# Recurrence of a hybrid encoder layer: order of the gram products, copies and decays around a chunk's slot, signs folded into copies, whole staging loads

## The chip, the cores and the metric

One Trainium2 chip, one core. The metric is device microseconds of one execution of the whole layer. The engines are TensorE (PE in the profile), VectorE (DVE), ScalarE (ACT), GpSimd (POOL) and SyncE (SP), which here only issues DMAs.

## What is computed

One encoder layer over 2048 tokens of 1024 channels. A combined projection feeds a bidirectional RWKV-7 time mixing (8 heads of 64) and a windowed attention; both are projected back, and a gated feed-forward follows. The change touches the recurrence of the first, which the reference writes step by step, for both directions:

```python
def rwkv7_step(S, inp):
    r, w, k, v, a, b = inp
    sa = jnp.einsum('dbhvk,dbhk->dbhv', S, a)
    S = S * w[..., None, :] + sa[..., None] * b[..., None, :] + v[..., :, None] * k[..., None, :]
    y = jnp.einsum('dbhvk,dbhk->dbhv', S, r)
    return S, y
```

with `a = -kk`, the negated and normalised key, and `b = iclr * kk`.

## The kernel before

The layer is a row of blocks: attention projections and attention, the RWKV projections, the gates, `recurrence_block`, then output projection, up and down. Only `recurrence_block` changes. It does the recurrence in chunks of 64 tokens (`L`), 32 chunks (`NCH`) for each direction `d`; direction 1 runs over the chunks from the back. Two heads lie in the two halves of the partitions, four such pairs (`RU`) side by side, so one tile of 128x256 elements holds a quantity of a chunk.

Inside a chunk the dependence of each token on the earlier ones is a triangular system. Its matrix (the "gram", products of the decayed `kk` with the grown `b`) is cut into 32x32 diagonal blocks and one off-diagonal block. The diagonal blocks of four chunks (`GROUP`), both directions and all heads are collected in `E`, transposed to `W` (`turn`), and solved together: `solve` on POOL makes 31 steps of a product and a sum on `W` and `V` (the first group is solved on DVE). `turn_back` transposes the inverses `V` into `upper` and `lower`. From them ACT's `spread` fills `Z` and `side` of a chunk with the masks `halves`, PE's `cross` and `corner` make the off-diagonal block of the inverse, and DVE's `merge` adds it to `Z`.

The loop `SLOTS` runs from -9 to 31, once on each engine, and the order within a slot is a list of stages written out by hand; each stage is called for both directions. In slot c an engine works on chunk c (`now`: the state work), c+1 (`ahead`: pair products, masks, inverse), c+8 (`front`: grams; `LAG` is 8) and c+9 (`after`: decays and growths). A slot in which c+1 is a multiple of four is called fresh: its chunk c+1 needs the group of inverses that is just being finished. Semaphores counted per stage (`done`) connect the engines.

- SP, `load`: six DMAs per direction bring the gates of chunk c+10 to `inp`; `load_raw` brings raw values to `toks` (only in the run-up, before slot 0), `load_v` the centred values, `store` writes the output.
- ACT: `x_copy`, `u_copy`, `spread`, `decay` (exp of the cumulated sum, to `dec`), `y_copy`, `tok_copy` (transposed keys), `growth`, `cross_copy`, `gram_copy`; in fresh slots `spread` stands after `y_copy`.
- POOL: `keys(f)` multiplies keys by `grow`, then a quarter of `solve`, for f = c+8.
- DVE: `scaled` (to `ar`, and the chunk's end decay to `dec_end`), `mask`, in fresh slots `turn_back`, then `state`, `state_decay`, `diagonal_a`, `diagonal_b`, `turn` once a group, `merge`.
- PE: `x_part`, `pairs_part`, `u_part`, `y_state`, `h_part`, `y_part`, `tok_part`, `cross`, `gram`, `corner`, and in the run-up `v_part`, which centres the raw values.

Of the kernel before, what the change touches and what calls it, by code (L numbers as in the profile page):

```python
# [7 lines left out]
ALU = mybir.AluOpType  # L8
ACT = mybir.ActivationFunctionType
# [12 lines left out]
RU = RW // P  # L22
R_TILES = 14
AH = 8
L = 64
# [11 lines left out]
MASK_COLS = dict(halves=2, both0=128, both1=128, running0=128, running1=128, centre=64)  # L37
# [11 lines left out]
def host_constants():  # L49
# [8 lines left out]
        halves=np.concatenate([s < 32, s >= 32], 1),  # L58
# [1017 lines left out]
def recurrence_block(nc, K):  # L1076
# [15 lines left out]
    LAG = 8  # L1092
# [9 lines left out]
    with ExitStack() as ctx:  # L1102
# [26 lines left out]
        raw_v = lambda d, r: toks[d][:, :, r % 2]  # L1129
# [81 lines left out]
        with nc.Block() as block:  # L1211
            @block.sync
            def _(sp):
# [20 lines left out]
                def load_raw(r):  # L1234
                    for d in DIRS:
                        done(sp, "v", d, r - 1)
                        sp.dma_start(raw_v(d, r), rkv_dram[:, at_chunk(r, d), 2 * RU * L:3 * RU * L].rearrange(
                            "p (m t) -> p m t", t=L)).then_inc(
                            S[parity("raw", r)][d], 16)
# [61 lines left out]
            def _(pe):  # L1301
# [132 lines left out]
                for c in SLOTS:  # L1434
                    now, ahead, front = live(c), live(c + 1), live(c + LAG)
                    for go, stage, n in ((now, x_part, c), (ahead, pairs_part, c + 1), (now, u_part, c),
                                         (now and c > 0, y_state, c), (now and c < NCH - 1, h_part, c),
                                         (now, y_part, c), (ahead, tok_part, c + 1),
                                         (ahead, cross, c + 1), (front, gram, c + LAG),
# [9 lines left out]
            def _(act):  # L1449
# [9 lines left out]
                def u_copy(c, d):  # L1459
                    done(act, "u", d, c + 1)  # L1460
                    done(act, "y", d, c - 1)
                    copy(stacked[d][HALVES[0], c % 2, :, 1], bank[d][0][HALVES[0], :, 0:L])
                    copy(stacked[d][HALVES[1], c % 2, :, 0], bank[d][0][HALVES[1], :, 0:L]).then_inc(
                        S["u_copied"][d], 1)

                def decay(f, d):
                    done(act, parity("in", f), d, 16 * LOADS * (f // 2 + 1))
                    done(act, "ar", d, f)
                    nc.scalar.activation(dec[d][:, :, 1:L + 1], given(d, f, "csum"), ACT.Exp,
                                         scale=-KAPPA).then_inc(S["dec"][d], 1)  # L1470
# [43 lines left out]
                def gram_copy(f, d):  # L1514
                    done(act, "diag_b", d, f + 1)
                    done(act, "cross", d, f - RING + 1)
                    copy(ring_g[d][:, f % RING, :, BL:L], bank[d][2][:, :, BL:L]).then_inc(S["g_copied"][d], 1)

                for c in SLOTS:
                    now, ahead, front, after = live(c), live(c + 1), live(c + LAG), live(c + LAG + 1)  # L1520
                    fresh = (c + 1) % GROUP == 0
                    for go, stage, n in ((now, x_copy, c), (now, u_copy, c), (ahead and not fresh, spread, c + 1),
                                         (after, decay, c + LAG + 1), (now, y_copy, c),
                                         (ahead and fresh, spread, c + 1), (ahead, tok_copy, c + 1),
# [1526 lines left out]
```

## Time and profile before

| what | value |
|---|---|
| three runs, median (lowest, highest) | 3045.7 us (3040.87, 3045.74) |
| the profiled execution: its time | 3042.19 us |
| its span, first to last instruction | 3040.4 us |
| granted TensorE clock, mean of the span | 0.951 |
| PE busy | 2711.5 us (89%) |
| DVE busy | 2057.7 us (68%) |
| ACT busy | 1361.1 us (45%) |
| POOL busy | 650.1 us (21%) |

The recurrence lies between about 838 and 1385 us of the span. Busy time is time in which an engine had an instruction in it; matmuls are pipelined, so a busy PE is not PE at its peak. A wait is charged to what released it last. Instructions of one kind are named by line, output and input.

### The profile page before, as it was taken

The numbers are of one execution on the slowest core, as the hardware profiler recorded it, in microseconds if no ns is written. First come the engines' busy times: TensorE is split into PE (matmuls) and PEld (weight loads), VectorE is DVE, ScalarE is ACT, GpSimd is POOL, SyncE is SP. The second block draws the span as 40 slices with busy tenths as digits, with TensorE's granted clock in tenths as the row PEclk, the third lists the DMA queues.
The fourth block names the chain that finished last, engine by engine and source line by source line (L and its number), as shares of the span: only waits on it lengthen the run. The fifth ranks groups of instructions, "written<-read, shape, count | busy, mean of one in ns | idle before, by whom it ended". The sixth has DMA issues, their size and how long they took to land. (4 is left out here: it accounts for less than half of the span.)

```text
span 3040.4 us, 54530 instructions
## 1 busy us (share of the span) xinstructions
PE 2711.5 (89%) x20738; PEld 2145.9 (71%) x20738; DVE 2057.7 (68%) x3080; ACT 1361.1 (45%) x2618; POOL 650.1 (21%) x779
## 2 busy tenths in 40 slices
PE   7889989998737888896989799999799999799999
PEld 4655578885436788784667578887588887588887
DVE  6877623235557676645446688888888887587786
ACT  4547711116624555454244444444544444344443
POOL 5447700000025778741331000000000000000000
PEclk9999999999968999998999899999899999899999
DMA  4442232324776444335653322222122221826401
GB/s 131 146 97 49 50 81 65 80 55 154 290 198 165 130 127 131 105 97 181 200 171 137 111 74 83 83 84 78 58 77 80 84 84 63 296 74 236 149 28 56
DMA packets 309771, 352.41 MB, mean 116 GB/s; under 512 B 123193, under 2 KB 213817, under 8 KB 309394
## 3 DMA queue, kind: packets, MB, share of 16 engines
q1 hardware_dynamic: 304626, 343.66, 36.1%
q10 hardware_dynamic: 4896, 5.38, 0.5%
q8 instruction: 162, 2.65, 0.4%
q14 instruction: 87, 0.71, 0.1%
HBM read 245.81 MB, written 103.14 MB: 115 GB/s over the span
## 5 line engine op out<-in xcount | busy, mean ns | idle before, releaser
L99 PE MATMUL up_p<-up_b_hi,up_a_hi 128*128 128x512 f32 x1232 | 491.2, 399 | 44.8 <-ACT inv L2304 22.2
L100 PE MATMUL up_p<-up_b_lo,up_a_hi 128*128 128x512 f32 x1232 | 491.0, 399 | 0.0
L101 PE MATMUL up_p<-up_b_hi,up_a_lo 128*128 128x512 f32 x1232 | 490.3, 398 | 0.0
L99 PEld LDWEIGHTS up_p<-up_b_hi,up_a_hi 128*128 128x128 f32 x1232 | 234.2, 190 | 106.0 <-ACT inv L2304 23.5
L100 PEld LDWEIGHTS up_p<-up_b_lo,up_a_hi 128*128 128x128 f32 x1232 | 234.0, 190 | 56.1
L101 PEld LDWEIGHTS up_p<-up_b_hi,up_a_lo 128*128 128x128 f32 x1232 | 234.0, 190 | 55.7
L2747 ACT CAST down_a_hi<-down_a 128x512 fp32r<-128x512 f32 x154 | 96.0, 624 | 262.4 <-PE down_p_x L101 145.2
L2259 ACT CAST up_a_hi<-up_a_sum 128x512 fp32r<-128x512 f32 x132 | 81.3, 616 | 217.6 <-DVE up_a_sum L2418 140.3
L2762 DVE TENSOR_TENSOR down_a_lo<-down_a,down_a_hi 128x512 fp32r<-128x512 f32 x154 | 106.4, 691 | 100.4 <-ACT down_a_hi L2747 100.4
L2329 ACT ACTIVATE up_con<-up_raw,vecs_sb 128x1023 f32<-128x1023 f32 (+1 forms) x88 | 109.7, 1246 | 126.0 <-DVE up_raw L2488 96.6
L2494 DVE SCALAR_TENSOR_TENSOR up_con<-up_raw,vecs_sb,up_con 128x1023 f32<-128x1023 f32 (+1 forms) x88 | 113.0, 1284 | 68.6 <-ACT up_con L2329 68.6
L99 PE MATMUL down_p_x<-down_b_hi,down_a_hi 128*128 128x512 f32 x352 | 138.9, 395 | 21.2 <-DVE down_b_lo L2764 21.1
L776 ACT COPY rwkv_project_raw_pad<-p_rwkv 128x512 f32<-128x512 f32 x56 | 32.9, 588 | 253.8 <-PE p_rwkv L93 253.8
L815 DVE TENSOR_SCALAR rwkv_project_mix<-rwkv_project_raw_pad,rwkv_project_keep 128x2048 f32<-128x2048 f32 x13 | 16.7, 1287 | 190.2 <-ACT rwkv_project_raw_pad L776 190.2
L100 PE MATMUL down_p_x<-down_b_lo,down_a_hi 128*128 128x512 f32 x352 | 138.2, 393 | 0.0
L101 PE MATMUL down_p_x<-down_b_hi,down_a_lo 128*128 128x512 f32 x352 | 138.0, 392 | 0.0
L595 POOL TENSOR_SCALAR attention_prob<-attention_prob,attention_inv 128x384 f32<-128x384 f32 (+1 forms) x96 | 117.2, 1238 | 57.4 <-DVE attention_inv L662 57.4
L2426 DVE TENSOR_TENSOR up_a_lo<-up_a_raw,up_a_hi 128x512 fp32r<-128x512 f32 x174 | 119.1, 685 | 12.8 <-ACT up_a_hi L2259 12.8
L1208 POOL TENSOR_TENSOR rec_V<-rec_V,rec_part 128x31 f32<-128x31 f32 (+15 forms) x217 | 123.2, 568 | 17.0
L1204 POOL TENSOR_TENSOR rec_part<-rec_W,rec_V 128x31 f32<-128x31 f32 (+15 forms) x217 | 115.3, 532 | 27.9 <-issue 11.8
L2426 DVE TENSOR_TENSOR up_a_lo<-up_a_sum,up_a_hi 128x512 fp32r<-128x512 f32 x132 | 91.4, 692 | 41.8 <-ACT up_a_hi L2259 32.6
L91 PE MATMUL mix_p_out<-mix_hi,mix_w_hi 128*128 128x512 f32 x256 | 108.7, 425 | 11.2 <-DVE mix_lo L1996 11.2
(289 smaller groups left out, 6939.4 us busy)
## 6 DMA issues: line engine op xcount, KB each, us to landing
up_a_raw<-in_w_up SPq DMA_DIRECT2D x172, 256.0 KB, 2.8
down_a<-in_w_down SPq DMA_DIRECT2D x88, 256.0 KB, 9.6
down_b<-act_out SPq DMA_DIRECT2D x88, 256.0 KB, 9.6
rec_inp<-gate_chunks SPq DMA_DIRECT2D x64, 256.0 KB, 3.3
rec_inp<-gate_chunks SPq DMA_DIRECT2D x256, 64.0 KB, 2.8
first_w<-in_w_attn SPq DMA_DIRECT2D x24, 512.0 KB, 3.5
rkv_chunks<-rwkv_project_mix SPq DMA_DIRECT2D x12, 1024.0 KB, 6.5
gate_chunks<-gates_out SPq DMA_DIRECT2D x3, 4096.0 KB, 12.2
```

The source lines that it names most:

```text
L91: pe.matmul(out, w_hi, x_hi, start=start, stop=False)
L99: pe.matmul(out, w_hi, x_hi, start=start, stop=False, skip_group_check=True)
L100: pe.matmul(out, w_hi, x_lo, start=False, stop=False, skip_group_check=True)
L101: return pe.matmul(out, w_lo, x_hi, start=False, stop=stop, skip_group_check=True)
L595: ops.tensor_scalar(prob[:, i % PB, lo:hi], prob[:, i % PB, lo:hi], inv[:, b % 2, h:h + 1], None, ALU.mult).then_inc(S[name], 1)
L1204: ops.tensor_tensor(product, W[:, below, b].unsqueeze(2).to_broadcast([P, n, b + 1]), V[:, b, cols].unsqueeze(1).to_broadcast([P, n, b + 1 ...
L1208: op = ops.tensor_tensor(V[:, below, cols], V[:, below, cols], product, ALU.add)
L2329: nc.scalar.activation(con[:, half, 0:count(g)], raw[:, half, cols(g)], ACT.Identity, scale=cw(1, half, g), bias=cb(half, g)).then_inc(S[f ...
L2426: tt(K.a_lo[i][:, :, :], of, f32(K.a_hi[i][:, :, :]), sub).then_inc(S[f"a_lo{i}"], 1)
L2494: stt(out=to, in0=raw[:, half, cols(g, -1)], scalar=cw(0, half, g), in1=to, op0=ALU.mult, op1=ALU.add).then_inc(S[f"tap1_{c}"], 1)
L2747: nc.scalar.copy(a_hi[:, s % 2], a_operand(i, k)).then_inc(S["a_hi"], 1)
L2762: tt(a_lo[:, s % 2], a_operand(i, k), a_hi[:, s % 2].bitcast(F32), sub).then_inc(S["a_lo"], 1)
```

## The change

- The negative sign of `a` leaves DVE's `scaled`, which now multiplies `kk` by the decay alone. It is put back in `u_copy` and `gram_copy` on ACT (a scale of -1) and in the diagonal blocks (masks `minus_halves`).
- The end decay `dec_end` is no longer a DVE copy out of `dec`; ACT makes it in `decay` with an exponential of its own over one column.
- PE: in fresh slots `gram` stands ahead of `y_part`; in others it stays behind `cross`.
- ACT: `y_copy` stands ahead of `decay`; in fresh slots `gram_copy` follows it, then `tok_copy`, `decay`, `growth`, and `spread` and `cross_copy` after these; in other slots `cross_copy` follows `y_copy`, then `tok_copy`, `decay`, `growth`, `gram_copy`.
- `raw_v` is laid out so that a staging load writes one run of 256 elements a partition instead of four of 64.
- The order of DVE's, POOL's and SP's stages is the same in both kernels.

```diff
-MASK_COLS = dict(halves=2, both0=128, both1=128, running0=128, running1=128, centre=64)
+MASK_COLS = dict(halves=2, minus_halves=2, both0=128, both1=128, running0=128, running1=128, centre=64)
...
-        halves=np.concatenate([s < 32, s >= 32], 1),
+        halves=np.concatenate([s < 32, s >= 32], 1), minus_halves=-1.0 * np.concatenate([s < 32, s >= 32], 1),
...
-        raw_v = lambda d, r: toks[d][:, :, r % 2]
+        raw_v = lambda d, r: toks[d][:, r % 2 * 2:r % 2 * 2 + 2].rearrange("p u h t -> p (u h) t")
...
-                        sp.dma_start(raw_v(d, r), rkv_dram[:, at_chunk(r, d), 2 * RU * L:3 * RU * L].rearrange(
-                            "p (m t) -> p m t", t=L)).then_inc(
+                        sp.dma_start(raw_v(d, r).rearrange("p m t -> p (m t)"),
+                                     rkv_dram[:, at_chunk(r, d), 2 * RU * L:3 * RU * L]).then_inc(
...
                     now, ahead, front = live(c), live(c + 1), live(c + LAG)
+                    fresh = (c + 1) % GROUP == 0
                     for go, stage, n in ((now, x_part, c), (ahead, pairs_part, c + 1), (now, u_part, c),
                                          (now and c > 0, y_state, c), (now and c < NCH - 1, h_part, c),
+                                         (front and fresh, gram, c + LAG),
                                          (now, y_part, c), (ahead, tok_part, c + 1),
-                                         (ahead, cross, c + 1), (front, gram, c + LAG),
+                                         (ahead, cross, c + 1), (front and not fresh, gram, c + LAG),
                                          (ahead, corner, c + 1)):
...
-                    copy(stacked[d][HALVES[0], c % 2, :, 1], bank[d][0][HALVES[0], :, 0:L])
-                    copy(stacked[d][HALVES[1], c % 2, :, 0], bank[d][0][HALVES[1], :, 0:L]).then_inc(
-                        S["u_copied"][d], 1)
+                    for h, rows in enumerate(HALVES):
+                        op = nc.scalar.activation(stacked[d][rows, c % 2, :, 1 - h], bank[d][0][rows, :, 0:L], ACT.Copy,
+                                                  scale=-1.0)
+                    op.then_inc(S["u_copied"][d], 1)
...
-                    nc.scalar.activation(dec[d][:, :, 1:L + 1], given(d, f, "csum"), ACT.Exp,
-                                         scale=-KAPPA).then_inc(S["dec"][d], 1)
+                    csum = given(d, f, "csum")
+                    nc.scalar.activation(dec_end[d][:, f], csum[:, :, (0 if d else L - 1)], ACT.Exp, scale=-KAPPA)
+                    nc.scalar.activation(dec[d][:, :, 1:L + 1], csum, ACT.Exp, scale=-KAPPA).then_inc(S["dec"][d], 1)
...
-                    copy(ring_g[d][:, f % RING, :, BL:L], bank[d][2][:, :, BL:L]).then_inc(S["g_copied"][d], 1)
+                    nc.scalar.activation(ring_g[d][:, f % RING, :, BL:L], bank[d][2][:, :, BL:L], ACT.Copy,
+                                         scale=-1.0).then_inc(S["g_copied"][d], 1)
...
                     for go, stage, n in ((now, x_copy, c), (now, u_copy, c), (ahead and not fresh, spread, c + 1),
-                                         (after, decay, c + LAG + 1), (now, y_copy, c),
-                                         (ahead and fresh, spread, c + 1), (ahead, tok_copy, c + 1),
-                                         (after, growth, c + LAG + 1), (ahead, cross_copy, c + 1),
-                                         (front, gram_copy, c + LAG)):
+                                         (now, y_copy, c),
+                                         (ahead and not fresh, cross_copy, c + 1),
+                                         (front and fresh, gram_copy, c + LAG), (ahead, tok_copy, c + 1),
+                                         (after, decay, c + LAG + 1), (after, growth, c + LAG + 1),
+                                         (ahead and fresh, spread, c + 1), (ahead and fresh, cross_copy, c + 1),
+                                         (front and not fresh, gram_copy, c + LAG)):
...
-                    nc.vector.scalar_tensor_tensor(out=ar[d][:, f % RING, :, 0:L], in0=given(d, f, "kk"),
-                                                   scalar=-1.0, in1=dec[d][:, :, 2 * d:2 * d + L],
-                                                   op0=ALU.mult, op1=ALU.mult)
-                    end = 1 if d else L
-                    nc.vector.tensor_copy(dec_end[d][:, f], dec[d][:, :, end])
+                    tt(ar[d][:, f % RING, :, 0:L], given(d, f, "kk"), dec[d][:, :, 2 * d:2 * d + L], ALU.mult)
...
-                    nc.vector.tensor_scalar(E[:, problems(f, d)], bank[d][2][:, :, 0:BL], half(0), None,
+                    nc.vector.tensor_scalar(E[:, problems(f, d)], bank[d][2][:, :, 0:BL], minus_half(0), None,
...
-                    nc.vector.scalar_tensor_tensor(out=E[:, at], in0=bank[d][2][:, :, BL:L], scalar=half(1),
+                    nc.vector.scalar_tensor_tensor(out=E[:, at], in0=bank[d][2][:, :, BL:L], scalar=minus_half(1),
```

## Rows read from the trace of the kernel before

**Rows 1.** Busy time by stretch: from:to, length, engines, granted clock, DMA share, GB/s.
```profile
932.00:1296.00 364.00, 305.00 (x7919) 289.61 (x7917) 250.98 (x516) 191.37 (x587) 275.08 (x434) 0.92 0.47 125
```

**Rows 2.** Waits, 760 to 1400: engine, line, releaser, us in total, times, longest.
```profile
DVE rec_E L1609 <- PE rec_bank L1410: 81.7, 41, 5.2
...
PE rec_bank L1307 <- ACT rec_side L1492: 44.2, 9, 6.9
...
PE rec_bank L1319 <- DMA rec_toks<-rkv_chunks: 33.4, 11, 6.7
```

**Rows 3.** Timeline of DVE, turn-backs one, seven and eight: start, us, line.
```profile
937.25 1.91 DVE L1629 STREAM_TRANSPOSE rec_upper<-rec_V 128x1024 f32<-128x1024 f32 x1
...
1286.71 1.91 DVE L1629 STREAM_TRANSPOSE rec_upper<-rec_V 128x1024 f32<-128x1024 f32 x1 [3.89 <-POOL rec_V L1208]
...
1338.13 1.96 DVE L1629 STREAM_TRANSPOSE rec_upper<-rec_V 128x1024 f32<-128x1024 f32 x1
```

**Rows 4.** Timeline of POOL around the fresh slot c = 11.
```profile
1111.73 0.25 POOL L1208 TENSOR_TENSOR rec_V<-rec_V,rec_part 128x31 f32<-128x31 f32 x1
1118.94 2.50 POOL L1540 TENSOR_TENSOR rec_bk<-rec_inp,rec_grow 128x512 f32<-128x512 f32 x2 [6.96 <-ACT rec_grow L1474]
...
1122.40 0.16 POOL L1192 MEMSET rec_V<- 128x32 f32 x1
1123.59 0.25 POOL L1204 TENSOR_TENSOR rec_part<-rec_W,rec_V 128x31 f32<-128x31 f32 x1 [1.03 <-issue]
...
1136.33 2.94 POOL L1540 TENSOR_TENSOR rec_bk<-rec_inp,rec_grow 128x512 f32<-128x512 f32 x2
```

**Rows 5.** Busy time by stretch, POOL alone: one group's solve, the last one's.
```profile
1123.50:1170.10 46.60, 41.93 (x68) 1.00 0.50 133
1298.20:1335.80 37.60, 32.81 (x62) 0.99 0.53 157
```

**Rows 6.** Timeline of DVE in the same fresh slot.
```profile
1116.21 0.75 DVE L1603 TENSOR_TENSOR rec_H<-rec_H,rec_dec_end 128x256 f32<-128x256 f32 x2
...
1120.80 0.60 DVE L1615 SCALAR_TENSOR_TENSOR rec_E<-rec_bank,rec_masks,rec_E 128x128 f32<-128x128 f32 x2
1121.48 1.97 DVE L1623 STREAM_TRANSPOSE rec_W<-rec_E 128x1024 f32<-128x1024 f32 x1
```

**Rows 7.** Timeline of ACT in the same fresh slot.
```profile
1115.74 0.69 ACT L1490 ACTIVATE rec_Z<-rec_upper,rec_masks 128x128 f32<-128x128 f32 x2 [6.50 <-DVE rec_lower L1630]
...
1117.51 1.04 ACT L1480 COPY rec_toks<-rec_bank 128x512 f32<-128x512 f32 x2
1118.45 0.72 ACT L1474 ACTIVATE rec_grow<-rec_inp 128x256 f32<-128x256 f32 x2
...
1121.17 0.53 ACT L1517 COPY rec_g<-rec_bank 128x128 f32<-128x128 f32 x2 [1.68 <-DVE rec_E L1615]
```

**Rows 8.** Groups by line and shape, 940 to 1390: count, busy us, mean ns, idle before.
```profile
L1574 DVE COPY rec_dec_end<-rec_dec 128x4 f32<-128x4 f32 x48 | 27.7, 577 | 0.0
...
L1517 ACT COPY rec_g<-rec_bank 128x128 f32<-128x128 f32 x50 | 13.1, 266 | 27.3 <-DVE rec_E L1615 27.2
```

**Rows 9.** Timeline of PE: fresh slot and the one after it.
```profile
1116.78 1.06 PE L1307 MATMUL rec_bank<-rec_side,rec_g 64*64 64x32 f32 x16 [6.93 <-ACT rec_side L1492]
...
1120.27 1.01 PE L1307 MATMUL rec_bank<-rec_Z,rec_low 64*64 64x32 f32 x16
...
1131.04 0.66 PE L1307 MATMUL rec_bank<-rec_side,rec_g 64*64 64x32 f32 x16 [0.45 <-ACT rec_ys L1498]
```

**Rows 10.** Busy time by stretch around PE's pause; the clock is third from the end.
```profile
1114.60:1121.30 6.70, 4.52 (x84) 4.53 (x86) 3.49 (x9) 3.88 (x13) 2.36 (x2) 0.50 0.47 130
```

**Rows 11.** DMA issues, 838 to 948: count, KB each, median us to landing.
```profile
rec_toks<-rkv_chunks SPq DMA_DIRECT2D x32, 128.0 KB, 2.8
...
rec_inp<-rkv_chunks SPq DMA_DIRECT2D x20, 128.0 KB, 3.1
```

**Rows 12.** Timeline of SP's DMA issues in the run-up and in the middle.
```profile
881.68 0.59 SPq L1231 DMA_DIRECT2D rec_inp<-rkv_chunks  x1
882.31 2.08 SPq L1237 DMA_DIRECT2D rec_toks<-rkv_chunks  x4
...
1111.80 0.44 SPq L1223 DMA_DIRECT2D rec_inp<-gate_chunks  x1
...
1115.47 2.51 SPq L1245 DMA_DIRECT2D rec_stacked<-v_chunks  x4
```

More of the change, by code:

```diff
@@ L1557, in _ @@
                 tt = nc.vector.tensor_tensor
-                half = lambda j: mask_of("halves")[:, j:j + 1]
+                minus_half = lambda j: mask_of("minus_halves")[:, j:j + 1]
                 STEPS = 2 * (BL - 1)
```

## Prediction

> **What bounds the kernel now.** The change touches only the recurrence, so I first looked at its busy time by stretch [rows 1]: after a run-up (838 to 932) comes a middle of 364 us, then a tail. No engine is full in the middle (PE 305 of 364 us, POOL 275), so shares don't say what binds. The list of waits does [rows 2]: PE waits 44 us for ACT's spread of the inverses, in 9 places. In the timelines those waits are one chain: POOL solves a group of four chunks, DVE turns the result back, ACT spreads it, PE goes on. The turn-backs come every 58.2 us (six periods, 937.25 to 1286.71, [rows 3]); a period is four slots.
>
> The timelines of one fresh slot (c+1 is a multiple of 4) show what the period is made of. I count from T, the end of POOL's solve at 1111.98 [rows 4]. POOL waits 6.96 us for the growth factors, forms the keys, clears V, and still waits for the turned gram matrices; its first product starts at T+11.6. From there to the next T it works without a real pause: 46.6 us [rows 5]. So the period is 11.6 + 46.6 = 58.2, and **POOL's round trip is the bound**: a microsecond counts if it lies between T and POOL's first product, or makes POOL wait inside the 46.6.
>
> What fills the 11.6 [rows 6, 7]: DVE turns back (3.7 us), ACT spreads (1.77), copies the transposed keys (0.94) and starts the growth at T+6.47; POOL's keys start 0.49 later. Keys and clearing take 3.62 us, so POOL is ready at T+10.6. Meanwhile PE has multiplied cross products, then grams, DVE has taken the diagonal blocks, and W is turned at T+11.45, the last to arrive. The two are only 0.9 us apart, so speeding up W alone is worth 0.9 at most.
>
> **DVE in a fresh slot.** The diff leaves DVE's order alone: turn-back, state, state decay, diagonals, turn. The grams now lie ahead of the output product on PE and are long done at T. The state decay ends at T+5.0 [rows 6]. The first pair of diagonals takes some 0.5 us, the second starts at T+5.4, the turn 0.68 later as before, and W is ready at T+8.1: 3.3 us earlier.
>
> **ACT in a fresh slot.** This decides. The gram copy now stands ahead of the transposed-key copy, the decays and the growth, and it waits for the second diagonal, which stands behind the turn-back. By the old distance (1120.80 to 1121.17, [rows 6, 7]) it starts at T+5.8. Then 0.5 for the two copies, 0.94 for the key copies, and the decays: 0.63 (the distance that a pair of exponentials takes, a little under its 0.72) plus two end decays of 4 elements a row. No row has one on ACT. Its nearest row is the copy of 128 elements at 266 ns [rows 8]; I take 0.15 each, because neighbours overlap, with bounds of 0.08 and 0.36, half of the full pair. Growth starts at 5.8+0.5+0.94+0.93 = T+8.15, keys at T+8.65, the first product at 8.65+3.62+0.05 = T+12.3. POOL no longer waits for W, but 1.7 us longer for growth: **+0.7 us a group** (bounds +0.5 and +1.2).
>
> **The next slot.** The spread of a fresh slot now comes behind the growth, at T+8.8, and the first cross product 1.04 later, at T+9.8 instead of T+4.8 [rows 7, 9]. Grams no longer stand between cross and corner (half of the 3.49 us from 1116.78 to 1120.27), so the next slot's first product starts near T+13.1 instead of T+9.8. The clock adds to it: in the row at 0.50 granted, 1.2 of 2.4 GHz [rows 10], PE comes out of a pause, and the row ends some 4.6 us after PE resumes. As long again reaches 1.5 us into the next slot's products, about 0.7 us dearer: 4.0 late in all. There the output copy stands ahead of the decays, which takes away PE's 0.45 wait for it: cross at 1131.04-T+4.0-0.5 = T+22.6. But ACT now copies the cross results first and waits for them (some 1.4 us), then key copies 0.94, decays 0.93, growth at T+25.9, keys at T+26.4. POOL is free for them at T+12.3+12.7 (1123.59 to 1136.33) = T+25.0: **+1.35 us a group** (bounds 0, if the clock is back and the copies slip into gaps, and 2.5). In the two slots after it PE needs about 11.7 us a slot and POOL 13.5, so the growths are early again.
>
> **End decays and sign off DVE.** DVE loses L1574, 577 ns a piece [rows 8], two a slot: 1.2 us. What hides it: before the diagonals DVE waits for grams (81.7 us, 41 times, [rows 2]), in fresh slots for POOL. Without that cover it would be 1.2 x 24 = 29 us. What can count is POOL's share in it. The bare solve takes 37.6 us in the last group, where no chunk is scaled; 46.6 with scaling and three key pairs of 2.5 to 2.9 (8.1 together), so scaling stretches POOL's work by 0.9, and the keys by up to 0.5 [rows 4, 5]: 1.4 in all. A third of the scaling instructions goes: -0.4 (bounds 0 and -1.4). The Trainium skill (SBUF — State Buffer, Who interferes with whom) says that a DVE copy in a two-port mode holds the port pair it shares with GpSimd, and that a product with two SBUF inputs contends too; L1574's 577 ns for 4 elements agree. If the copy were all of the contention, this term would be -1.4. Signs in ACT's copies change nothing in their size.
>
> **Raw staging whole.** 32 loads of 128 KB go from 256-byte to 1-KB runs. The loads of the same size and the new shape (L1231) land in 3.1 us against 2.8 and take 0.59 us to issue against 2.08 for four [rows 11, 12]. The run-up is paced by SP, which issues some 7.3 us of other loads a slot (twice the 3.67 from 1111.80 to 1115.47, [rows 12]). Bounds: 32 x 0.08 = +2.6, and -3 (a tenth of the 33.4 us that PE waits for these landings, [rows 2]). With the copies gone from between a load and SP's next one: -1 for the run-up.
>
> **Last group and tail.** After the sixth period there are no keys; that period is 51.4 us (to 1338.13, [rows 3]), where POOL's solve has ended and DVE's mask is last. No growth stands ahead of the spread there, PE starts about 1.8 late and wins back 0.15 in each of some five slots in which the cross copy moves ahead: +1.
>
> **Sum.** 6 x (0.7+1.35-0.4) = +9.9, last +1, run-up -1: +9.9. The profiled execution took 3042.2 us (3040.4 of span and 1.8 around it), so 3052.1; the three runs have their median at 3045.7, 3.5 above it, so I give 3055.5.
>
> **Rivals.** (1) The next slot's wait is hidden: a group costs +0.3, in all +2 to +5: 3048 to 3051. For it: the 1.35 is a small difference of long sums. Against: cross is 5 us later, which is a plain row. (2) The port: POOL gets back all 1.4 a group and the next slot's wait is at its lower bound: 6 x (0.7-1.4) = -4.2, run-up -3: 3038.5. It decides once the port returns more than the late growth takes. For it: 577 ns where 4 elements are moved; against: two thirds of those instructions stay. (3) PE's chain becomes the bound: it was 2 to 5 us ahead of T and loses 4. If its slots don't shorten below 13 us, it sets T and adds 2 us a group, +12: 3067. (4) W early pays in full, the growth no later than before: 11.6 becomes 10.6, -6 in all, 3039.5. That needs ACT's gram copy not to wait behind the turn-back; the code says it does.
>
> **Chances.** Forecast (3050 to 3063) 0.50; rival 1 0.23; rival 2 0.09; rival 3 0.12; rival 4 0.06. A measurement of this kernel can tell about 0.2%, 6 us. Slower by more: most of the forecast and rival 3, 0.56; within: 0.29; faster: 0.15. The range leaves out rivals 2 and 4 and the far end of 3: 3043 to 3066.
>
> **What would show it.** In fresh slots: W turned at T+8.1; POOL's keys at T+8.6 with growth as the last wait; first product at T+12.3; cross at T+9.8; the next slot's keys waiting on growth too; periods near 59.9 us. DVE more idle before the diagonals. I am wrong if keys start before T+8, if the 46.6 shrinks by over 1 us, or if the run-up moves by over 3.

## The result

| | before | after |
|---|---|---|
| median of six runs each, same chip | 3045.13 us (3038.86 to 3047.49) | 3055.94 us (3052.70 to 3063.06) |
| profiled execution | 3042.19 us, span 3040.41 | 3052.70 us, span 3050.92 |
| granted clock, mean | 0.951 | 0.946 |

The changed kernel is slower: the medians differ by 10.8 us, and the ratio after/before is 1.0045, 95% interval 1.0035 to 1.0055, which is 13.7 us (10.7 to 16.7). The prediction gave 3055.5 us, 9.8 above the median of 3045.7 that it started from. In the profiled execution the span is 10.5 us longer, but the recurrence alone, from its first instruction to its last, is 15.7 us longer (546.2 to 561.9); the parts around it, which the change doesn't touch, were 1.8 and 3.4 us shorter in this execution. So part of the agreement is luck, and the next sections are about the recurrence.

Busy time by stretch of the changed kernel (the columns of [rows 1]): the run-up, the middle, the tail.
```profile
836.00:929.00 93.00, 40.07 (x755) 37.94 (x757) 53.39 (x125) 28.16 (x95) 25.35 (x22) 0.62 0.73 210
929.00:1293.00 364.00, 301.19 (x7678) 285.94 (x7676) 244.71 (x454) 190.37 (x618) 267.34 (x421) 0.90 0.46 123
1293.00:1398.00 105.00, 93.90 (x2488) 88.96 (x2486) 48.18 (x89) 52.52 (x151) 39.69 (x76) 0.95 0.28 81
```
In as many microseconds as in [rows 1] every engine has done less, so all of them wait longer. The list of waits says where (760 to 1410, line, releaser, us in total, times, longest):
```profile
POOL rec_bk L1547 <- ACT rec_grow L1478: 136.4, 20, 13.7
...
PE rec_bank L1307 <- ACT rec_side L1496: 63.8, 9, 10.4
...
DVE rec_E L1612 <- PE rec_bank L1410: 54.7, 29, 4.8
...
PE rec_bank L1319 <- DMA rec_toks<-rkv_chunks: 30.3, 8, 7.0
```
PE waits 20 us longer for the spread than in [rows 2]. POOL's wait for the growth was already its longest in the recurrence before the change (115.8 us in 14 places); it is 20.6 us longer and stands in six places more. DVE's wait for grams is shorter than in [rows 2], 54.7 us instead of 81.7. The turn-backs (first and seventh; before in [rows 3]) come every 60.88 us instead of 58.24:
```profile
934.30 1.90 DVE L1632 STREAM_TRANSPOSE rec_upper<-rec_V 128x1024 f32<-128x1024 f32 x1
...
1299.58 1.93 DVE L1632 STREAM_TRANSPOSE rec_upper<-rec_V 128x1024 f32<-128x1024 f32 x1 [3.61 <-POOL rec_V L1208]
```
The same fresh slot as in [rows 4, 6, 7, 9]; here T, the end of POOL's solve, is 1115.88. POOL:
```profile
1115.63 0.25 POOL L1208 TENSOR_TENSOR rec_V<-rec_V,rec_part 128x31 f32<-128x31 f32 x1
1124.33 2.50 POOL L1547 TENSOR_TENSOR rec_bk<-rec_inp,rec_grow 128x512 f32<-128x512 f32 x2 [8.44 <-ACT rec_grow L1478]
...
1128.01 0.25 POOL L1204 TENSOR_TENSOR rec_part<-rec_W,rec_V 128x31 f32<-128x31 f32 x1
...
1142.97 3.00 POOL L1547 TENSOR_TENSOR rec_bk<-rec_inp,rec_grow 128x512 f32<-128x512 f32 x2 [2.41 <-ACT rec_grow L1478]
```
ACT:
```profile
1121.64 0.54 ACT L1521 ACTIVATE rec_g<-rec_bank 128x128 f32<-128x128 f32 x2 [5.80 <-DVE rec_E L1618]
1122.07 1.07 ACT L1484 COPY rec_toks<-rec_bank 128x512 f32<-128x512 f32 x2
1123.01 0.23 ACT L1473 ACTIVATE rec_dec_end<-rec_inp 128x4 f32<-128x4 f32 x1
1123.12 0.43 ACT L1474 ACTIVATE rec_dec<-rec_inp 128x256 f32<-128x256 f32 x1
...
1123.83 0.72 ACT L1478 ACTIVATE rec_grow<-rec_inp 128x256 f32<-128x256 f32 x2
1124.44 0.69 ACT L1494 ACTIVATE rec_Z<-rec_upper,rec_masks 128x128 f32<-128x128 f32 x2
...
1140.07 0.27 ACT L1516 COPY rec_low<-rec_bank 128x128 f32<-128x128 f32 x1 [0.76 <-PE rec_bank L1307]
...
1142.47 0.73 ACT L1478 ACTIVATE rec_grow<-rec_inp 128x256 f32<-128x256 f32 x2
```
DVE and PE, and the granted clock (third from the end) over PE's slow stretch:
```profile
1121.27 0.59 DVE L1618 SCALAR_TENSOR_TENSOR rec_E<-rec_bank,rec_masks,rec_E 128x128 f32<-128x128 f32 x2
1121.95 1.93 DVE L1626 STREAM_TRANSPOSE rec_W<-rec_E 128x1024 f32<-128x1024 f32 x1
```
```profile
1125.48 1.06 PE L1307 MATMUL rec_bank<-rec_side,rec_g 64*64 64x32 f32 x16 [9.04 <-ACT rec_side L1496]
...
1132.47 2.06 PE L1385 MATMUL rec_bank<-rec_ar,rec_bk 64*128 64x128 f32 x32
...
1139.37 0.66 PE L1307 MATMUL rec_bank<-rec_side,rec_g 64*64 64x32 f32 x16
```
```profile
1118.70:1132.40 13.70, 6.92 (x128) 6.93 (x128) 7.49 (x16) 5.57 (x19) 7.23 (x14) 0.50 0.25 67
```
W is turned at T+8.0 (1121.95 + 1.93), 3.5 us earlier than before, and nobody uses that: the gram copy starts at T+5.8, so growth at T+7.95, POOL's keys at T+8.45, the first product at T+12.1. Before, it was T+11.6. The spread follows the growth, the cross products come at T+9.6, and PE, idle for 9.04 us, comes back at half clock and stays there for 6.9 us, to T+16.5, through the next slot's first products. There the growth starts at T+26.6 and POOL stands 2.41 us before its keys. How late PE is there shows in the first products of that slot and its L1385, before and after:
```profile
1121.67 0.31 PE L1307 MATMUL rec_bank<-rec_H,rec_ar 64*64 64x64 f32 x4
...
1123.66 2.06 PE L1385 MATMUL rec_bank<-rec_ar,rec_bk 64*128 64x128 f32 x32
```
```profile
1128.93 0.46 PE L1307 MATMUL rec_bank<-rec_H,rec_ar 64*64 64x64 f32 x4
```
Before, the slot's first products start at T+9.7 and L1385 1.99 us later, at T+11.7. After, they start at T+13.05, and L1385 (above) comes 3.54 us later, at T+16.6: 3.4 us late at the start, and 1.55 more because they run at half clock.

The terms of the sum over the six periods, from such timelines of each of them:

| term | predicted | measured in the recurrence |
|---|---|---|
| first product later | +4.2 | +2.0 (T+12.1 in five, T+10.8 in the first) |
| next slot's wait for growth | +8.1 | +14.5 (2.60, 1.99, 2.40, 2.41, 2.58, 2.53) |
| port relief in POOL's stretch | -2.4 | -0.7 (46.66 to 46.54 a group) |
| last group and tail | +1 | +1.0 (seventh period +1.6, tail -0.6) |
| run-up | -1 | -1.1 (98.96 to 97.82) |
| sum | +9.9 | +15.7 |

The later comparisons give a hint whether the medians or the recurrence come nearer to the cost. The kernel before, run again beside the experiments, had medians of 3041.0, 3041.1 and 3042.4 us (31, 29 and 17 runs), and in all ten other kernels below (11 sets of runs) the median less the length of the profiled recurrence is 2490 to 2495 us. After: 3055.9 - 561.9 = 2494.0. Against 3041 to 3042 the change costs 13.5 to 15 us, and the ratio of the first comparison, 13.7 us, agrees. The changed kernel was not run again beside them, so this stays a hint. Ratios below are to the kernel before, on the same chip, with a 95% interval.

### The profile page after: what moved, and what is told of

Its sections match the earlier page's. It is cut to its first block and busy times, and to the rows that moved or that the text cites. A ratio compares the mean times of both kernels' runs of the same rounds, so it can differ in the third digit from the quotient of the medians.

```text
span 3050.9 us, 54530 instructions
## 1 busy us (share of the span) xinstructions
PE 2716.7 (89%) x20738; PEld 2153.6 (71%) x20738; DVE 2055.1 (67%) x3016; ACT 1368.1 (45%) x2682; POOL 648.4 (21%) x779
## 5 line engine op out<-in xcount | busy, mean ns | idle before, releaser
L815 DVE TENSOR_SCALAR rwkv_project_mix<-rwkv_project_raw_pad,rwkv_project_keep 128x2048 f32<-128x2048 f32 x13 | 16.7, 1287 | 192.1 <-ACT rwkv_project_raw_pad L776 192.1
## 6 DMA issues: line engine op xcount, KB each, us to landing
gate_chunks<-gates_out SPq DMA_DIRECT2D x3, 4096.0 KB, 13.5
```

## Experiments: which part of the order costs

**The other slots' growth ahead of the cross copies.** The changed kernel, but for slots that aren't fresh; the fresh slot stays as changed.
```diff
+                (after and not fresh, decay, c + LAG + 1), (after and not fresh, growth, c + LAG + 1),
                 (ahead and not fresh, cross_copy, c + 1),
                 (front and fresh, gram_copy, c + LAG), (ahead, tok_copy, c + 1),
-                (after, decay, c + LAG + 1), (after, growth, c + LAG + 1),
+                (after and fresh, decay, c + LAG + 1), (after and fresh, growth, c + LAG + 1),
```


> The changed kernel, but in slots that are not fresh ACT takes decays and growths right behind the output copy, ahead of the cross and key copies. Fresh slots as changed. My theory (POOL waits 2.4 us a group for the growth of the slot after a fresh one, which stands behind copies that wait for PE's late cross products): growths then start about 3 us earlier, POOL's second keys of a group start without a wait near T+24.8, the period falls from 60.9 to about 58.5 us, in all 6 x 2.4 = 14 us faster than the changed kernel, level with the kernel before (3042 to 3048 us). Rival (the wait is set by PE's chain, which is late by itself, or the port makes POOL slow): the keys wait as before, the period stays above 60 us and the time at 3053 to 3058.

Measured: 3045.76 us, ratio 1.0014 [1.0001, 1.0028]. The first product stays at T+12.2, the next slot's wait is gone in four periods and 0.5 and 0.8 us in two, the period 58.69. POOL, with T at 1110.54:
```profile
1119.12 2.50 POOL L1549 TENSOR_TENSOR rec_bk<-rec_inp,rec_grow 128x512 f32<-128x512 f32 x2 [8.58 <-ACT rec_grow L1478]
1135.30 2.50 POOL L1549 TENSOR_TENSOR rec_bk<-rec_inp,rec_grow 128x512 f32<-128x512 f32 x2
```
The second row has no idle time before it. The six periods together are 13.2 us shorter than in the changed kernel, so nearly all of the 14.5 us of the next slot's wait comes back. The recurrence is 552.7 us long, 9.2 shorter: its seventh period and its tail were 5.0 us longer, its run-up 1.0 shorter.

**The spread back in front.** The changed kernel, with the fresh slot's spread ahead of the gram copy as before; the other slots stay as changed.
```diff
                 (ahead and not fresh, cross_copy, c + 1),
+                (ahead and fresh, spread, c + 1),
                 (front and fresh, gram_copy, c + LAG), (ahead, tok_copy, c + 1),
                 (after, decay, c + LAG + 1), (after, growth, c + LAG + 1),
-                (ahead and fresh, spread, c + 1), (ahead and fresh, cross_copy, c + 1),
+                (ahead and fresh, cross_copy, c + 1),
```


> The changed kernel, but in fresh slots ACT's spread is back in front of the gram copy, so it runs from T+3.7 as before. Theory: the spread's lateness (T+8 instead of T+3.7) is what makes the next slot late. First product stays near T+12.2 (the growth still waits for the gram copy), the next slot's growth comes 4 to 5 us sooner, the wait there (2.4 us) goes, period 58.6 us, 3043 to 3046. Rival (that wait comes from ACT's order in the next slot alone, key copies and cross copies ahead of the growth): it stays above 1.5 us and the period above 60.

Measured: 3043.36 us, 1.0003 [0.9992, 1.0013]; no wait in five periods, 1.0 in one; 58.45 us a period. PE (T at 1109.80), then POOL:
```profile
1114.57 1.06 PE L1307 MATMUL rec_bank<-rec_side,rec_g 64*64 64x32 f32 x16 [4.66 <-ACT rec_side L1496]
...
1123.40 2.06 PE L1385 MATMUL rec_bank<-rec_ar,rec_bk 64*128 64x128 f32 x32
```
```profile
1118.23 2.49 POOL L1548 TENSOR_TENSOR rec_bk<-rec_inp,rec_grow 128x512 f32<-128x512 f32 x2 [8.43 <-ACT rec_grow L1478]
1134.49 2.86 POOL L1548 TENSOR_TENSOR rec_bk<-rec_inp,rec_grow 128x512 f32<-128x512 f32 x2
```
Cross at T+4.8, the next slot's row L1385 at T+13.6 instead of T+16.6. So the wait needs both: a late spread in the fresh slot, and a growth queued behind the cross copies in the next. Each edit alone takes it away.

**The fresh slot's growth early.** The changed kernel, decay and growth in the fresh slot right behind the output copy, ahead of the gram copy.
```diff
                 (now, y_copy, c),
+                (after and fresh, decay, c + LAG + 1), (after and fresh, growth, c + LAG + 1),
                 (ahead and not fresh, cross_copy, c + 1),
                 (front and fresh, gram_copy, c + LAG), (ahead, tok_copy, c + 1),
-                (after, decay, c + LAG + 1), (after, growth, c + LAG + 1),
+                (after and not fresh, decay, c + LAG + 1), (after and not fresh, growth, c + LAG + 1),
```


> The changed kernel, but in fresh slots ACT takes decays and growths right behind the output copy, ahead of the gram copy; the other slots as changed. Theory: keys no longer wait behind the turn-back, they run from T on, and the first product starts near T+6.1 (W turned at T+6.0 to 8.1) instead of T+12.1; the spread comes 1.4 us earlier. But POOL then reaches the next slot's keys 6 us sooner than their growth, so the wait there grows from 2.4 to about 6.8 us: period near 59.4 us, 9 us faster than the changed kernel (3045 to 3049). Rival (the two places are independent): the period falls by all 6 us to 55 us and the time to about 3020. Second rival (ACT's order in fresh slots doesn't matter since something else holds the keys): the first product stays at T+12.

Measured: 3051.65 us, 1.0032 [1.0017, 1.0048]. The first product comes at T+6.9 to T+9.6, 3.6 us earlier on average and not the 6 expected: from the second period on W, turned at T+8.0 to T+9.5, is what comes last. The next slot takes 2.6 of the 3.6 back, and the time misses the expected 3045 to 3049. POOL, T at 1112.55:
```profile
1115.99 2.68 POOL L1549 TENSOR_TENSOR rec_bk<-rec_inp,rec_grow 128x512 f32<-128x512 f32 x2 [3.44 <-ACT rec_grow L1478]
1139.49 2.99 POOL L1549 TENSOR_TENSOR rec_bk<-rec_inp,rec_grow 128x512 f32<-128x512 f32 x2 [5.08 <-ACT rec_grow L1478]
```
4.6 to 5.5 us of wait there, a period of 59.64. With the late spread PE's chain sets the next slot's growth, whenever POOL is ready.

**Grams early, and nothing else.** The kernel before with PE's new order.
```diff
+                (front and fresh, gram, c + LAG),
                 (now, y_part, c), (ahead, tok_part, c + 1),
-                (ahead, cross, c + 1), (front, gram, c + LAG),
+                (ahead, cross, c + 1), (front and not fresh, gram, c + LAG),
```


> The kernel before with one part alone: PE takes the grams ahead of the output product in fresh slots. Theory: W is turned 3 us earlier, POOL's last wait becomes the growth at T+6.5, the first product starts at T+10.65 instead of T+11.55, and nothing else gets later: period 57.3 us, 5 to 6 us faster than before (3039 to 3041). Rival (grams ahead of the output product push PE's chain back and eat it): period 58.2, no change.

Measured: 3035.29 us, 0.9980 [0.9969, 0.9992]: faster. First product at T+10.6 to T+10.8 in all six periods, no wait in the next slot, 57.46 us a period. PE's pause is 3.5 us instead of 6.9, but what follows it no longer has the grams in it, and in this slot its slow stretch is 10.1 us instead of the 6.7 of [rows 10]; busy time in that stretch:
```profile
1112.00:1122.10 10.10, 8.15 (x136) 7.90 (x138) 6.53 (x18) 4.83 (x16) 6.04 (x11) 0.50 0.42 115
```

**The gram copy in front, on top of that.** The same kernel, with ACT's gram copy of the fresh slot behind the spread and ahead of key copies and growth.
```diff
-                (ahead and fresh, spread, c + 1), (ahead, tok_copy, c + 1),
-                (after, growth, c + LAG + 1), (ahead, cross_copy, c + 1),
-                (front, gram_copy, c + LAG)):
+                (ahead and fresh, spread, c + 1), (front and fresh, gram_copy, c + LAG),
+                (ahead, tok_copy, c + 1), (after, growth, c + LAG + 1), (ahead, cross_copy, c + 1),
+                (front and not fresh, gram_copy, c + LAG)):
```


> The kernel before with PE's early grams (as before_gram_early, first product at T+10.6), and one more part: in fresh slots ACT's gram copy stands ahead of the key copies and the growth, the spread still first. Theory (the gram copy waits for the diagonals behind the turn-back and holds back the growth): gram copy near T+5.8, growth near T+7.2 instead of T+6.5, first product at T+11.4, +0.8 us a group against before_gram_early, period 58.2 and no gain over the kernel before. Rival (the gram copy finds its diagonal done and costs its 0.5 us alone, or nothing): first product at T+10.6 to 11.0.

Measured: 3041.66 us, 0.9999 [0.9989, 1.0008], 58.27 us a period. POOL without the gram copy in front (T 1108.47) and with it (T 1112.75):
```profile
1115.46 2.50 POOL L1542 TENSOR_TENSOR rec_bk<-rec_inp,rec_grow 128x512 f32<-128x512 f32 x2 [6.98 <-ACT rec_grow L1476]
```
```profile
1120.47 2.50 POOL L1543 TENSOR_TENSOR rec_bk<-rec_inp,rec_grow 128x512 f32<-128x512 f32 x2 [7.72 <-ACT rec_grow L1476]
```
The copy costs 0.74 us a group on POOL's path, and takes the whole gain of the early grams (6 us) with it.

## Experiments: the small parts

**Signs and end decays off VectorE alone**, in the kernel before (the changed decay, the two negative copies, the negative masks and the plain product; orders and staging as before).
```diff
-                    nc.vector.scalar_tensor_tensor(out=ar[d][:, f % RING, :, 0:L], in0=given(d, f, "kk"),
-                                                   scalar=-1.0, in1=dec[d][:, :, 2 * d:2 * d + L],
-                                                   op0=ALU.mult, op1=ALU.mult)
-                    end = 1 if d else L
-                    nc.vector.tensor_copy(dec_end[d][:, f], dec[d][:, :, end])
+                    tt(ar[d][:, f % RING, :, 0:L], given(d, f, "kk"), dec[d][:, :, 2 * d:2 * d + L], ALU.mult)
```


> The kernel before with one part alone: signs in ACT's copies and masks, end decays made by ACT, no copy and a plain product on VectorE. Orders and staging as before. Theory (VectorE has slack, the port costs POOL little): POOL's 46.7 us between first product and the end of the solve shrink by 0.1 to 0.4 us, the period is 57.8 to 58.2, the time 0 to 3 us below before. Rival (the copy's hold on the shared port is most of POOL's stretching): 1.4 us a group, 8 us faster.

Measured: 3040.51 us, 0.9996 [0.9985, 1.0007]. POOL's stretch is 46.22 us on average (0.44 less), the period 57.86. Where VectorE's saving went is seen in its groups by line and shape (count, busy us, mean ns, idle before), in the kernel before and in the changed kernel:
```profile
L1570 DVE SCALAR_TENSOR_TENSOR rec_ar<-rec_inp,rec_dec 128x256 f32<-128x256 f32 x48 | 30.2, 630 | 0.0
...
L1575 DVE TENSOR_TENSOR rec_ar<-rec_inp,rec_dec 128x256 f32<-128x256 f32 x48 | 19.7, 411 | 0.0
```
```profile
L1578 DVE TENSOR_TENSOR rec_ar<-rec_inp,rec_dec 128x256 f32<-128x256 f32 x48 | 40.9, 853 | 0.0
...
L1577 DVE TENSOR_TENSOR rec_ar<-rec_inp,rec_dec 128x256 f32<-128x256 f32 x48 | 35.0, 730 | 0.0
```
Before, product, copy [rows 8], product took 630 + 577 + 411 = 1618 ns; in the changed kernel the two products take 730 + 853 = 1583, and in this experiment 695 + 886 = 1581. The second product has doubled though its line did not change. Four rows of the changed kernel show why; POOL forms keys from 1142.97 to 1145.97 (above):
```profile
1142.68 0.41 DVE L1577 TENSOR_TENSOR rec_ar<-rec_inp,rec_dec 128x256 f32<-128x256 f32 x1
1143.01 0.42 DVE L1578 TENSOR_TENSOR rec_ar<-rec_inp,rec_dec 128x256 f32<-128x256 f32 x1
1143.35 1.50 DVE L1577 TENSOR_TENSOR rec_ar<-rec_inp,rec_dec 128x256 f32<-128x256 f32 x1
1144.76 1.49 DVE L1578 TENSOR_TENSOR rec_ar<-rec_inp,rec_dec 128x256 f32<-128x256 f32 x1
```
The same instruction takes 0.41 or 0.42 us, or 1.49 to 1.50 beside POOL's keys (the one at 1143.01 starts with the keys and is not stretched yet). Before, the copy was one of those that stood there. Since taking it out leaves the sum as it was, its 577 ns were mostly a wait, and the wait has passed to its neighbour. By the rule of the Trainium skill (SBUF — State Buffer, Who interferes with whom) a VectorE instruction with two SBUF inputs contends with a GpSimd instruction that reads SBUF; the trace agrees, 1.49 against 0.41 us.

**Raw staging whole alone**, in the kernel before (the two edits of the staging's view and its load).
```diff
-                        sp.dma_start(raw_v(d, r), rkv_dram[:, at_chunk(r, d), 2 * RU * L:3 * RU * L].rearrange(
-                            "p (m t) -> p m t", t=L)).then_inc(
+                        sp.dma_start(raw_v(d, r).rearrange("p m t -> p (m t)"),
+                                     rkv_dram[:, at_chunk(r, d), 2 * RU * L:3 * RU * L]).then_inc(
```


> The kernel before with one part alone: the raw staging loads whole (one 1-KB run a partition). Theory: they land in about 3 us and take 0.43 to 0.6 us to issue, SP paces the run-up as before; from the recurrence's first instruction to the first turn-back 99 us plus or minus 1.5, nothing else moves; time the same within 3 us. Rival (short runs congest the DMA engines, whose share is 0.78 there): the run-up falls by more than 3 us.

Measured: 3041.30 us, 0.9997 [0.9986, 1.0007]. The run-up is 97.1 us, 0.4 below the range expected for it, against 98.96 in the kernel before and 98.3 to 99.6 in the three other kernels with the old staging; with the new one it is 96.4 to 100.2. Neither the run-up nor the total tells them apart. In the changed kernel's rows of DMA issues (838 to 948; 836 to 948 there) the loads land after 3.0 us, against 2.8 in [rows 11]; in this experiment they land after 2.6. The landing has no clear direction either:
```profile
rec_toks<-rkv_chunks SPq DMA_DIRECT2D x32, 128.0 KB, 3.0
```

## Experiments: a version that is faster than both

**Growth at no cost.** The changed kernel with the first order of ACT in the slots that aren't fresh, and in fresh slots growth first, then spread, the gram copy last.
```diff
                 (ahead and not fresh, spread, c + 1),
+                (after and not fresh, decay, c + LAG + 1), (now, y_copy, c),
+                (after and fresh, decay, c + LAG + 1), (after and fresh, growth, c + LAG + 1),
+                (ahead and fresh, spread, c + 1), (ahead, tok_copy, c + 1),
+                (after and not fresh, growth, c + LAG + 1), (ahead, cross_copy, c + 1),
+                (front, gram_copy, c + LAG)):
-                (now, y_copy, c),
-                (ahead and not fresh, cross_copy, c + 1),
-                (front and fresh, gram_copy, c + LAG), (ahead, tok_copy, c + 1),
-                (after, decay, c + LAG + 1), (after, growth, c + LAG + 1),
-                (ahead and fresh, spread, c + 1), (ahead and fresh, cross_copy, c + 1),
-                (front and not fresh, gram_copy, c + LAG)):
```


> A new version: the changed kernel's PE order, signs, end decays and staging; ACT's order as in the kernel before, except that in fresh slots decays and growths come ahead of the spread, before T. Theory: POOL forms its keys from T on, the first product waits only for W, at T+8.1; the next slot's growth is at hand (spread not late); period 8.1 + 46.3 = 54.4 us, 23 us faster than before (about 3018), unless PE's chain, 50.8 us in the group without keys, binds first. Rival (POOL isn't the bound after all, PE's chain is): the period stays above 57.

Measured: 3025.07 us, 0.9939 [0.9917, 0.9961]; run again under its second name:

> The same kernel as growth_at_no_cost, timed again beside the one above: 15 to 19 us faster than the kernel before, period 56.1 us.

3027.74 us, 0.9956 [0.9943, 0.9968]. 56.1 us a period in both. That is less than was expected (a period of 54.4 and about 3018 us), though well below the rival's 57. From the second period on the keys start at T+2.2 to T+3.8 in the first run and not at T, because they still wait for ACT's growth. In four of the first run's six periods the first product comes at T+9.7 to T+10.0, not at the T+8.1 expected. DVE, T at 1103.80:
```profile
1103.84 1.97 DVE L1631 STREAM_TRANSPOSE rec_upper<-rec_V 128x1024 f32<-128x1024 f32 x1 [1.42 <-POOL rec_V L1208]
...
1108.17 2.31 DVE L1605 TENSOR_TENSOR rec_H<-rec_H,rec_dec_end 128x256 f32<-128x256 f32 x2
...
1111.61 1.94 DVE L1625 STREAM_TRANSPOSE rec_W<-rec_E 128x1024 f32<-128x1024 f32 x1
```
The state decay takes 2.31 us instead of the 0.75 of [rows 6]. POOL's keys have moved from behind it to beside it (1107.53 to 1110.21 there), and W comes at T+9.8.

**Diagonals before the turn-back.** Growth at no cost, with DVE's fresh slot in the order diagonals, turn-back, turn, state, state decay.
```diff
+                    for go, stage, n in ((front and fresh, diagonal_a, c + LAG), (front and fresh, diagonal_b, c + LAG)):
+                        if go:
+                            for d in DIRS:
+                                stage(n, d)
                     if ahead and fresh:
                         turn_back((c + 1) // GROUP)
+                    if front and fresh:
+                        turn((c + LAG) // GROUP)
-                    for go, stage, n in ((carry, state, c), (carry, state_decay, c),
-                                         (front, diagonal_a, c + LAG), (front, diagonal_b, c + LAG)):
+                    for go, stage, n in ((carry, state, c), (carry, state_decay, c),
+                                         (front and not fresh, diagonal_a, c + LAG),
+                                         (front and not fresh, diagonal_b, c + LAG)):
```


> The version above, and VectorE in fresh slots takes the diagonal blocks ahead of the turn-back (the grams are there by then) and turns W right behind it, ahead of state and decay. Theory: W is ready near T+5.8, first product T+5.9, period 52.3 us, 36 us faster than before (about 3005); PE's chain, at some 51 us, is then nearly as long. Rival (state and decay, 1.9 us later, hold the next slot's PE work): the period stays at 54 or above.

Measured: 3037.07 us, 0.9982 [0.9972, 0.9992]: 5 us a period more than expected (57.56). The first product comes 5.7 us behind the turn-back's start, but the turn-back itself starts 1.5 to 3.7 us behind POOL's solve, since DVE now waits for grams before it, and the next slot waits 2.2 to 3.2 us:
```profile
1113.23 2.52 POOL L1546 TENSOR_TENSOR rec_bk<-rec_inp,rec_grow 128x512 f32<-128x512 f32 x2 [4.74 <-ACT rec_grow L1478]
...
1132.92 2.51 POOL L1546 TENSOR_TENSOR rec_bk<-rec_inp,rec_grow 128x512 f32<-128x512 f32 x2 [3.19 <-ACT rec_grow L1478]
```
Here PE's chain, rival 3 of the prediction, has become a bound beside POOL. The period is where this experiment's own rival put it (54 or above), but its cause is not the one: state and decay come last in the next kernel too, and there POOL waits only 0.4 to 0.6 us in the slot after from the second period on.

**Turn-back first, state last.** Again growth at no cost, with DVE's fresh slot in the order turn-back, diagonals, turn, state, state decay; the lines of state and state decay as in the edit above.
```diff
                     if ahead and fresh:
                         turn_back((c + 1) // GROUP)
+                    for go, stage, n in ((front and fresh, diagonal_a, c + LAG), (front and fresh, diagonal_b, c + LAG)):
+                        if go:
+                            for d in DIRS:
+                                stage(n, d)
+                    if front and fresh:
+                        turn((c + LAG) // GROUP)
...
```


> The version with growth at no cost, and VectorE in fresh slots takes diagonals and the turn right behind the turn-back, state and state decay after them. In that version the state decay ran 2.3 us instead of 0.75 while POOL formed keys, and W came at T+9.8. Theory (the two collide on the port): with the diagonals first W is turned near T+7, first product T+7.1, period 53.5 us, or about 55 where PE's chain binds; 10 us or more faster than that version. Rival (PE's chain was the bound there already): period 56, same time.

Measured: 3023.05 us, 0.9941 [0.9927, 0.9956], 54.70 us a period; first product at T+6.9 to T+8.1. DVE, T at 1100.27:
```profile
1104.51 0.60 DVE L1617 SCALAR_TENSOR_TENSOR rec_E<-rec_bank,rec_masks,rec_E 128x128 f32<-128x128 f32 x2
1105.20 1.98 DVE L1625 STREAM_TRANSPOSE rec_W<-rec_E 128x1024 f32<-128x1024 f32 x1
...
1107.73 0.76 DVE L1605 TENSOR_TENSOR rec_H<-rec_H,rec_dec_end 128x256 f32<-128x256 f32 x2
```
W at T+6.9, the state decay at 0.76 again. The six periods together are 8 us shorter than with growth at no cost, the seventh is 4 longer (55.4): POOL's last solve is over 11 us before DVE turns it back, because DVE is held by PE's results of the slots before. Of the 8 us, 2 to 5 are left in the total, where 10 or more were expected. It is the fastest of these kernels, 19 us ahead of the one before.

## Why the prediction came out right, and where it did not

- **POOL's round trip is the bound.** Right. In all six periods the turn-back starts 0.03 us behind the solve, and period = first product + stretch still holds: 12.1 + 48.9 = 61.0.
- **W early, growth late.** Right in order and size: W T+8.0 (said 8.1), gram copy T+5.8 (5.8), growth T+7.95 (8.15), keys T+8.45 (8.65), first product T+12.1 (12.3). The price was +0.5 instead of +0.7 a group: the gram copies took 0.43 us (said 0.5) and the decays 0.82 (said 0.93), since an end decay takes 225 ns but occupies ACT for 0.11 us from its start to the next (said 0.15). Grams early and the gram copy in front were then measured apart: -0.9 and +0.74. Rival 4 is refuted for this change, and the early grams alone show what it described.
- **The next slot.** The mechanism was right, the size too small: this is the term that failed, 2.42 against 1.35 us a group, at its upper bound of 2.5. The prediction took it that the clock's slow stretch would reach as far past PE's return as before (4.6 us), which made the next slot's first products 0.7 us dearer and put the slot 4.0 us late. These products did start at T+13.05 (said 13.1), but the stretch reached 6.9 us past the return and covered them whole: they were 1.55 dearer, and the slot was 4.9 late at PE's L1385 (T+16.6 for T+11.7). The 4.6 was read in one slot: over the six fresh slots from the second turn-back to the seventh the kernel before has a reach of 4.6 to 8.0 us. In the changed kernel the wait goes with the reach: 1.99 us at a reach of about 6.0, and 2.40, 2.41, 2.53 and 2.58 at 6.9, 7.0, 7.2 and 7.5. Cross came at T+23.5 for 22.6, growth at T+26.6 for 25.9. With POOL free at T+24.7 for 25.0 the wait comes to 2.4. Rival 1 is refuted, and the spread put back in front shows that it would have been true with the cross products at T+4.8.
- **End decays and signs.** VectorE was to save 1.2 us a slot and POOL 0.4 us a group; the saving was to be covered by VectorE's waits. VectorE saved 0.07 us a slot (2 x 35 ns), POOL 0.1 in the changed kernel and 0.44 alone. With the waits covering it the first error did no harm. The prediction took the copy's 577 ns as a sign that it holds the port; the rows above show it waiting for POOL instead. Rival 2 (a relief of 1.4 us a group) is refuted. One sign failed here: DVE was to be more idle before the diagonals, and it waited 54.7 us there instead of 81.7.
- **Raw staging, last group, tail.** Within what a run can tell: -1.1 and +1.0 for -1 and +1. The staging alone moves nothing that can be told from the scatter, so its -1 is not shown.
- **The total.** 3055.5 (3055.6 by its own terms) against 3055.9 is closer than its terms were, and that is luck: in the profiled executions the recurrence lost 15.7 us instead of 9.9, and the median of the kernel before that the estimate was added to, of three runs, was some 4 us above the 3041 to 3042 of its later runs. That these two offset each other is the likely account; the later runs lack the changed kernel.
- **Rival 3**, PE's chain, did not bind here, but is close: it does with the diagonals before the turn-back, and in the seventh period of the fastest kernel.
- **Not settled.** What of PE's work or pause sets the length of the slow stretch. Around c = 11 it was 6.7 us after a pause of 6.9 with grams behind it, 10.1 after 3.5 without them, 13.7 after 9.0 without them, but it differs from slot to slot in one kernel (see the last section), and no run changed the pause alone.

## What to carry to other kernels

A late instruction in an in-order queue costs at each place where it is waited for: follow it one slot further than the slot that was edited, and read what clock PE has there, in every such slot and not in one: here one slot's reach of 4.6 us stood for a range of 4.6 to 8.0. Speeding up the last of two arrivals is worth only their distance (0.9 us here), and an order that puts a wait for the second in front of the first gives even that back. A stretched small instruction beside a contending engine may be a wait and not work; take it out and the next one waits.

## What the runs showed of the hardware that was not expected

- PE's return from a pause was not at one price, nor one that goes by the pause. Around c = 11 the clock stood at 0.50 for 6.7 us with a pause of 6.9 (before), 10.1 with 3.5 (early grams alone), 10.2 with 4.7 (spread back in front), 13.7 with 9.0 (changed). In all four it fell while PE was idle. But one slot doesn't rank the kernels. Over the six fresh slots from the second turn-back to the seventh it was 6.8 us in four and 10.2 in two before, 10.2 in four, 6.8 in one and 3.5 in one with the early grams alone, and 13.7 in three and 10.2 in three in the changed kernel. The raw staging alone, which leaves PE's order as it was, had 6.8 in two and 10.2 in four. Three kernels with a late spread (the changed one, the other slots' growth early, the fresh slot's growth early) had 13.7 in seven of 18 and 10.2 in the rest. Three with grams ahead and the spread early (early grams alone, gram copy in front, spread back in front) had 10.2 in 11 of 18 and 13.7 in one. The three kernels with grams behind the pause (before, signs and end decays alone, raw staging alone) had 6.8 in 12 of 18. So grams ahead of the pause go with 10.2 instead of 6.8, and 13.7 goes with the late spread.
- A VectorE product of 256 columns takes 0.41 us alone and up to 1.50 beside POOL's keys, and a state decay of two such products 2.31 instead of 0.75. Before the change L1575 was never above 0.414 us in 48 executions; the likely reason is that the copy ahead of it took the wait.
- A scalar exponential of 4 elements a row lasts 225 ns and holds the next one up by 0.11 us.
